# Moving the statistics of the time steps under the last projection tiles, and the rows of decay sums under the backward scan

## What is computed

```python
dt = jax.nn.softplus(dt_raw + dt_bias)
a = dt * (-jnp.exp(a_log))
acum = jnp.cumsum(ac, axis=2)
seg = acum[:, :, :, None] - acum[:, :, None, :]
lmat = jnp.exp(jnp.where(tril, seg, -jnp.inf))
y_diag = jnp.einsum('bclsge,bcsgep->bclgep', cb[..., None] * lmat, xc)
decay_to_end = jnp.exp(acum[:, :, -1:] - acum)
states = jnp.einsum('bcsgn,bcsgep->bcgepn', bc, decay_to_end[..., None] * xc)
```

## Time and profile before

| | |
|---|---|
| median of three runs | 3931.37 us |
| the profiled execution | 3925.94 us, its span 3924.3 us |
| PE busy | 3614.0 us (92%) |
| DVE, ACT, POOL busy | 2146.7, 1360.7, 1594.6 us |
| mean granted TensorE clock | 0.957 of 2.4 GHz |
| DMA | 521.87 MB, mean 133 GB/s |

### The profile page before, as it was taken

The page is one execution under the profiler, slowest core; times in us unless marked ns, Lnnn a source line. Parts: engine busy times, 40 slices in busy tenths (PEclk is TensorE's granted clock), DMA queues, the critical chain, the costliest instruction groups (busy, mean ns, idle before and its releaser), DMA issues. The chain is left out here.

```text
span 3924.3 us, 57718 instructions
## 1 busy us (share of the span) xinstructions
PE 3614.0 (92%) x20917; PEld 2850.7 (73%) x20917; DVE 2146.7 (55%) x4515; ACT 1360.7 (35%) x3566; POOL 1594.6 (41%) x1471
## 2 busy tenths in 40 slices
PE   6899999998875999899989998999999997899998
PEld 5777777887753667677767776677777775788887
DVE  2262145206414664366436653788888887465554
ACT  2122112212110003212322123778778885222222
POOL 5336342453505666567666664424233332100000
PEclk9999999999987999999999999999999998999999
DMA  4424422422314654634453342745544544444443
GB/s 166 150 77 138 170 77 72 136 94 64 102 40 160 212 166 137 209 122 136 128 185 120 122 142 89 172 125 136 137 127 114 139 132 128 162 158 154 166 152 103
DMA packets 366864, 521.87 MB, mean 133 GB/s; under 512 B 27595, under 2 KB 257555, under 8 KB 363859
## 3 DMA queue, kind: packets, MB, share of 16 engines
q1 hardware_dynamic: 329683, 402.80, 32.6%
q0 software_dynamic: 27456, 94.78, 8.1%
q10 hardware_dynamic: 9472, 20.97, 1.5%
HBM read 334.18 MB, written 184.29 MB: 132 GB/s over the span
## 5 line engine op out<-in xcount | busy, mean ns | idle before, releaser
L1713 ACT ACTIVATE attn_p_sb<-attn_p_sb,attn_o_sb 128x256 f32<-128x256 f32 (+1 forms) x1152 | 535.0, 466 | 183.7 <-DVE attn_o_sb L1747 178.2
L235 POOL TENSOR_TENSOR front_w_hi<-front_w_raw,one 128x1024 fp32r<-128x1024 f32 (+1 forms) x96 | 165.9, 1728 | 566.0 <-PE front_out L432 532.2
L1747 DVE CUSTOM_DVE_ANT_0 attn_p_sb<-attn_s_ps,attn_mask 128x256 f32<-128x256 f32 (+1 forms) x1152 | 368.8, 376 | 43.9 <-PE attn_s_ps L1646 43.7
L1067 PE MATMUL late_out<-h_hi,late_w_hi 128*128 128x512 f32 x1152 | 344.5, 443 | 22.5 <-issue 22.5
L1537 POOL COPY attn_q_apart<-attn_q 128x128 f32<-128x128 f32 (+2 forms) x256 | 136.9, 535 | 523.9 <-PE attn_s_ps L1646 517.5
L1067 PEld LDWEIGHTS late_out<-h_hi,late_w_hi 128*128 128x128 f32 x1152 | 225.0, 197 | 119.6 <-issue 78.4
L369 DVE TENSOR_SCALAR front_acc<-front_chan,front_consts 128x1024 f32<-128x1024 f32 (+2 forms) x36 | 38.8, 1077 | 473.3 <-ACT front_chan L281 473.3
L1186 ACT COPY late_m<-late_seg 128x512 f32<-128x512 f32 x96 | 55.9, 583 | 680.4 <-PE late_seg L1088 671.1
L1067 PE MATMUL late_out<-h_hi,late_w_lo 128*128 128x512 f32 x1152 | 286.7, 391 | 0.0
L1067 PE MATMUL late_out<-h_lo,late_w_hi 128*128 128x512 f32 x1152 | 284.5, 389 | 0.0
L1659 PE MATMUL attn_pt_ps<-ident,attn_p_sb 128*128 128x128 f32 x1920 | 278.4, 282 | 0.4 <-ACT attn_p_sb L1713 0.4
(11 more groups left out here) (211 smaller groups left out, 7380.1 us busy)
## 6 DMA issues: line engine op xcount, KB each, us to landing
front_w_raw<-w_in POOLq DMA_DIRECT2D x84, 512.0 KB, 4.1
output_parts<-s_o SPq DMA_DIRECT2D x24, 1584.0 KB, 6.5
late_w_raw<-w_in POOLq DMA_DIRECT2D x144, 256.0 KB, 3.9
s_o<-attn_o_sb SPq DMA_DIRECT2D x128, 264.0 KB, 3.0
late_xb<-s_xb SPq DMA_DIRECT2D x48, 640.0 KB, 5.8
s_zs<-front_stage SPq DMA_DIRECT2D x48, 256.0 KB, 2.0
s_v<-front_stage SPq DMA_DIRECT2D x48, 256.0 KB, 2.2
s_states<-late_state SPq DMA_DIRECT2D x24, 512.0 KB, 3.3
```

The costliest lines, as they stand in the source:

```text
L235: nc.gpsimd.tensor_tensor(hi, raw, one.to_broadcast([P, 2, cols]), ALU.mult).then_inc(sem["w_split"], 1)
L1067: last = nc.tensor.matmul(out[u][:, :], w[s][:, k, :], h[:, k, half], start=first, stop=h is h_lo and k == KT - 1)
L1713: last = nc.scalar.activation(cut, cut, ACT.Exp, scale=-1.0, bias=o_sb[g // 4 % ring][:, g % 4, h, VW:OW], accum_out=o_sb[g // 4 % ring][: ...
L1747: last = nc.vector.tensor_tensor_reduce(out=p_sb[g % 4][:, h, 0:width], in0=s_ps[g % 2][h][:, 0:width], in1=mask[:, step.pattern.strip(ste ...
```

## The change

- `ssd_stats_phase` and `decay_rows_phase` are gone as stages. dt stays on chip: it is no longer stored and loaded back.
- The statistics are computed in front_phase under the v units of the last block: DVE's part after its last work there, ACT's and PE's in single steps after named units (`STATS`, `SUMS`). Constant masks are set by POOL ahead of load 8. The four small loads of `dt_bias` and `a_log` go to SP's queue at the start. Results lie where x tiles and the norm's gain lay.
- The rows of sums are made in the backward slots: 12 rounds of 4 transposes instead of 6 of 8. Round r is filled by DVE in slot r + 2, turned by PE and copied by ACT in slot r + 3, split by DVE and stored by SP in slot r + 4.
- late_phase begins on POOL with the weights. The table of ones is made in five steps in slots 5, 7, 9, 11, 13. POOL weighs the first x between the first and the second weight. SP loads the rotation table ahead of the second x; `gain` and `skip` follow in slot 8.
- In slots 0 to 23 PE and DVE do the unit first and then the scan.
- The states of the backward scan go through three tiles instead of two.

```diff
+STATS = {("v", 0, 1): "exp", ("v", 0, 2): "log", ("v", 0, 6): "log_dt",
+         ("v", 1, 2): "decay", ("v", 1, 3): "entry", ("v", 1, 4): "total"}
+SUMS = {("v", 1, 0): 0, ("v", 1, 1): 1, ("v", 1, 2): 2}
...
             for load in range(BLOCKS * len(groups)):
+                if load == len(groups):
+                    set_masks()
...
+            def stats(what):
+                if what == "exp":
+                    act.wait_ge(sem["stats_in"], 16 * 2 * DIR)
+                    nc.scalar.activation(rate[:, :], a_log[:, :], ACT.Exp).then_inc(sem["stats_act"], 1)
...
+            def sums(i):
+                pe.wait_ge(sem["masks_set"], 9)
+                pe.wait_ge(sem["a_ready"], 1)
...
+                for d in range(DIR):
+                    last = nc.tensor.matmul((rest, upto, whole)[i][d], lhs[d], heads(a, d), start=True, stop=True)
...
-                    sp.dma_start(scratch["dt"][first:first + BLOCK, :].rearrange("(t p) n -> p t n", p=P),
-                                 dt_toks[:, :, :]).then_inc(sem["dt_stored"], 16)
...
-def ssd_stats_phase(nc, sem, c, params, scratch, st):
...
-def decay_rows_phase(nc, sem, c, scratch, st):
...
             fetch(0)
             fetch(1)
-            for w in range(2):
-                split(w)
+            split(0)
             weigh(0)
+            split(1)
             for slot in range(len(units)):
                 if slot + 1 < first_forward:
                     weigh(slot + 1)
+                if slot in (5, 7, 9, 11, 13):
+                    select_rows((slot - 5) // 2)
...
+            def store_rows(r):
+                sp.wait_ge(sem["wide_split"], r + 1)
...
             load_back(0)
+            sp.dma_start(table[:, :, :], t_in["rope"][:, :, BLOCK:]).then_inc(sem["l_rope_in"], 16)
             load_back(1)
...
                     store_back(slot)
+                    if 0 <= slot - first_round - 2 < rounds:
+                        store_rows(slot - first_round - 2)
...
+            def turn_rows(r):
+                pe.wait_ge(sem["wide_steps"], r + 2)
...
+                for k in range(4):
+                    last = nc.tensor.transpose(seg[r % 2][:, k * P:(k + 1) * P],
+                                               wide[r % 2][:, k, :, :].rearrange("p d n -> p (d n)"), c["ident"][:, :])
...
             for slot, unit in enumerate(units):
-                scan(slot)
-                multiply(unit)
+                if slot < first_forward:
+                    multiply(unit)
+                    scan(slot)
+                else:
+                    scan(slot)
+                    multiply(unit)
...
             def back_step(j):
                 dve.wait_ge(sem["b_state"], state_ready(j))
-                if j:
-
-                    dve.wait_ge(sem["b_stored"][1 - j % 2], 16 * ((j + 1) // 2))
...
+                if j >= 2:
+
+                    dve.wait_ge(sem["b_stored"][(j + 1) % 3], 16 * ((j + 1) // 3))
...
+            def fill_rows(r):
...
+                for part in range(2):
+                    last = nc.vector.tensor_copy(wide[r % 2][:, :, :, part * HEADS:(part + 1) * HEADS],
+                                                 source[:, first:first + 4, :].rearrange("p c (d h) -> p c d h", d=DIR))
...
+            def split_rows(r):
+                dve.wait_ge(sem["wide_high"], r + 1)
...
+                nc.vector.scalar_tensor_tensor(row_out[r % 2].bitcast(F32R), row_high[r % 2].bitcast(F32),
+                                               st["low_row"][:, :], seg[r % 2][:, :], ALU.mult, ALU.add
...
                 if slot < first_forward:
+                    if slot == first_round - 1:
+                        nc.vector.memset(y[:, :], 0.0).then_inc(sem["wide_steps"], 1)
...
+                    if 0 <= slot - first_round - 2 < rounds:
+                        split_rows(slot - first_round - 2)
+                    if 0 <= slot - first_round < rounds:
+                        fill_rows(slot - first_round)
                     back_step(slot)
```

More of the change, by code:

```diff
@@ L334, in _ @@
                     take_dt_back(unit, units[unit.n - 1].event)
+                if unit.b == BLOCKS - 1 and (unit.name, unit.part, unit.j) in STATS:
+                    stats(STATS[unit.name, unit.part, unit.j])
                 t = next_tile(unit)
@@ L467, in _ @@
                     turn_dt_back(unit, units[unit.n - 1].event)
+                if unit.b == BLOCKS - 1 and (unit.name, unit.part, unit.j) in SUMS:
+                    sums(SUMS[unit.name, unit.part, unit.j])
                 t = next_tile(unit)
@@ L774, in late_phase @@
     quads = HEADS // 4
+    rounds = 2 * NT // 4
+    first_round = 2
     units = late_units()
@@ L833, in state_ready, with rows_stored_before @@
             return j + 1 + (j >= turned_over)
+        def rows_stored_before(r):
+            return sum(DIR if x >= rounds // 2 else 1 for x in range(r % 2, r, 2))
         def part_of(slot):
@@ L965, in load_rows @@
                     sp.wait_ge(sem["f_rows_set"], 6)
+                    for u in range(2):
+                        sp.wait_ge(sem["sums_stored"][u], 16 * rows_stored_before(rounds + u))
                 sums = scratch["sums"].rearrange("(d q h) (c l) -> c d q h l", d=DIR, q=2, l=P)
@@ L1083, in decays @@
                     pe.wait_ge(sem["f_rows_in"], 48 * (n + 1))
+                    pe.wait_ge(sem["wide_split"], rounds)
                 pe.wait_ge(sem["f_m_steps"], n * (quads + 1) + q)
@@ L1163, in _ @@
         def _(act):
-            act.wait_ge(sem["f_rows_set"], 5)
-            nc.scalar.copy(rows[:, :, :], m[:, :, :]).then_inc(sem["f_rows_set"], 1)
             def load_h(turn, half):
@@ L1208, in _ @@
             for slot, unit in enumerate(units):
+                if 0 <= slot - first_round - 1 < rounds:
+                    high_rows(slot - first_round - 1)
+                if slot == first_round + rounds + 2:
+                    act.wait_ge(sem["f_rows_set"], 5)
+                    nc.scalar.copy(rows[:, :, :], m[:, :, :]).then_inc(sem["f_rows_set"], 1)
                 n, part = part_of(slot)
```

379 lines of the change are left out of this document (168 added, 211 removed).

## The result

The changed kernel takes 3897.62 us (median of 5 runs, 3883.20 to 3904.55), the kernel before 3931.37 in the same comparison: ratio 0.9912 [0.9898, 0.9926], 33.8 us saved where 57.7 were forecast. It is faster, and lies outside the range on the slow side. The profiled execution is the median one (span 3896.0 us).

A forecast was written before the change was run, and what follows sets the result against it. PE was taken to set the pace on both sides of its 86.1 us gap. Saving 67.4 at the begin, less 5.2 (rows), 2.5 (state load) and 2 (stalls), gave 57.7 us: 3931.4 to 3873.7 us, range 3853 to 3893.

The forecast's parts named there:

- the gap: PE's 86.1 us between front products and backward slots: predicted to become one stretch of some 12 to 18 us.
- three groups of sums: PE's statistics sums left after the last v units: 12 records at full clock, 3.9 us.
- the third tile: Third tile for the backward scan's states: worth nothing and costing nothing.
- the turning: PE's 12 rounds of four row transposes in the backward slots: 5.2 us given back, 10.4 at half clock.
- rival 2: POOL becomes the bound: weights late in slots 5 to 13, 15 us; 38 to 46 saved, near 3889; chance 0.17.
- rival 1: PE's stalls on DVE's state vanish in the backward slots: 70 to 79 us saved, near 3857; chance 0.15.
- rival 3: DVE's row copies collide with POOL every round, about 5 us each, 61 us: slower than before; chance 0.02.
- Begin: Last front product through slot 2: 42.2 us against 109.6, so 67.4 us saved, bounds 58 to 70.5.
- Slots 3 to 23: Backward slots: row transposes cost 5.2 us and stalls on DVE's state 2 us more.
- The stalls on DVE's state: 19 us lost in slots 3 to 23: pattern stays, 2 us more; bounds all 19 gone or 19 more.
- which unit stands between two `add_back`s: Unit before scan in backward slots only shifts this, 5.44 us in either order.
- Slot 25: After slot 24, PE waits for the backward state's load: 2.5 us lost, 0 if faster, 5 if the clock falls.

The follow-up runs named there:

- loads_in_turn: Changed kernel with the rotation table loaded after the first two weight pieces and chunk 0's states loaded ahead of x; 3887.62 us, ratio 0.9899.
- turned_in_psum: Changed kernel with the rotated halves of units 0 to 21 in two free PSUM banks instead of SBUF; 3869.86 us, ratio 0.9833.
- select_in_idle: Changed kernel with POOL's table of ones made in slots 2, 6, 10, 14, 18 instead of 5, 7, 9, 11, 13; 3886.34 us, ratio 0.9883.
- scan_first: Changed kernel with PE and DVE doing the scan before the unit in the backward slots, as before the change; 3884.95 us, ratio 0.9885.
- all five edits: Changed kernel with rotated halves in PSUM, selects moved, stores early, row copies on ACT, two loads later; 3856.22 us unit first, 3865.05 scan first.

## Why the prediction was right and wrong

**Right:** the gap was the place to gain, it was one stretch with one begin (14.6 us, within 12 to 18), DVE's and ACT's steps hid under v, three groups of sums took 4 us of PE, the third tile was worth nothing, the turning cost PE the 5.2 us taken (156.9 against 162.3 us of slots, with the old order and the rotation in PSUM, is 5.4). Of the rivals none came: PE waits for no low part of a weight in slots 5 to 13 (rival 2), stalls on the state are left (rival 1), and the copies cost PE only the two waits of 5.0 us (rival 3).

**Begin, 67.4 forecast, 57.0 measured: a mis-sized sum.** The weight's landing, taken as 5 us, was 8.46, near the bound of 8.9 from the table's own row; loads_in_turn shows that the table beside it costs 2.64 of it. Slots 0 to 2, 30 us from the landing, took 1196.8 - 1161.99 = 34.8; turned_in_psum, 6.6 us shorter from the first product on, shows that DVE's held rotation is the reason. The last front product ended 1.6 us later than the sums explain (the kernel before's own front code ended up to 3.1 us later in other kernels' profiles, so this need not be the change's), and the drain was 0.5 us longer: 3.5 + 4.8 + 1.6 + 0.5 = 10.4.

**Slots 3 to 23, 7.2 us more forecast, 13.1 measured: the step that failed.** Under "The stalls on DVE's state" the question "Does this stay?" was answered from L1258 alone, as POOL's doing, with 2 us for the new work; they grew by 7.9. And the order was to shift only "which unit stands between two `add_back`s". Both steps looked at PE and at one line of DVE. The rotation's second pair of operations also has two operands in SBUF, and in the kernel before 13.4 of the 19.1 us went when one of them was put into PSUM. The order matters as well: it decides whether PE waits for POOL's weighing, and what stands ahead of `back_step` on DVE. By the runs:

- the new order alone: 19.1 to 15.5 us, a gain of 3.6;
- with rows, copies and selects in slots 2, 6, ... (select_in_idle): 17.5;
- selects in the odd slots 5 to 13, as changed: 27.0, so 9.5 us for the place of five pieces of POOL's work (7.7 with the rotation in PSUM).

The prediction named these pieces, and looked only for a weight behind them. With the old order all of the new work would have cost 0.9 us (scan_first, 20.0 against 19.1): the 2 us taken fit an order that the change doesn't keep.

The Trainium skill (SBUF — State Buffer, section "SBUF: two separate sides") lists, beside the fp32 copy that the prediction cited, a VectorE operation with two SBUF inputs against a GpSimd operation that reads SBUF. The rows agree: L1238 takes 33.9 us for 21 operations with two; with one in PSUM 20 of them take 6.9 + 6.8 = 13.7. Applied to every line of DVE in the slots, the rule would have led to L1249 of the kernel before.

**Slot 25, 2.5 forecast, 6.3 measured: mis-sized.** PE waits 3.44 us, and then works at a granted clock of 0.60 (the mean of 1391.2 to 1397.2; 3.62 us for four products that take 1.88 at full clock). The upper end named, 5 for a fall of the clock, was nearer. loads_in_turn takes it away.

These make 10.4 + 5.9 + 3.8 = 20.1 us. By the medians 57.7 - 33.8 = 23.9 us are missing. The parts, however, are read from two profiled executions, which are only 28.3 us apart, so that 29.4 are missing there. Of the other 9.3 us 8.5 lie in the forward slots, whose code is the same, and 0.8 behind late_phase. From unit 29 to the end of late_phase the profiled execution of before took 965.1 us, that of the changed kernel 975.0. The other kernels took 967.2 to 975.7, and those made from the kernel before 966.0, 966.1 and 974.9, so that the kernel before's own code reaches either end. Whether a small part of this is the change's stays open.

## What to carry to other kernels

Before moving work, list every operation of the busy elementwise engine with both operands in SBUF, next to what POOL does in the same stretch: a wait is named after the last of them, here `back_step`, while the rotation before it had a share that its own length doesn't show. Put one operand into a free PSUM bank (13 and 14 us of slots here, in the two kernels) and long POOL work into slots in which POOL waits anyway (8 to 9.5 us). An order is not good or bad by itself: unit first won 3.6 and 4.5 us of slots in the kernel before and 5.4 with all five edits, and lost 7.0 and 6.9 with POOL's selects in the odd slots.

## What the runs showed of the hardware

A DVE operation that POOL holds up isn't always let in when POOL's instruction ends: the first of the two copies above lasts through a product of 1.91 us and the select of 2.01 us behind it, and L1248 at 1188.64 through two products of POOL. Nor is it only the one that comes second that waits, as the prediction read the earlier trace rows: the five long L1258 of the kernel before begin 0.63 us ahead of L886, each while POOL issues a fetch (at 1298.14 in the earlier trace rows, the issue from 1297.96 to 1298.75), and still last 4.63 us each, through L886 and the split behind it. POOL's instructions are held as well, less: the select of 2.0 us took 2.48 beside L1238. With an operand in PSUM no plain addition or multiplication (TENSOR_TENSOR) of 512 columns lasted over 0.70 us, and none of 1024 over 1.23, in these slots of the 18 profiled executions. And a 256 KB weight, landing 3.6 us after its issue in the median of the eight fetched up to 1188 us, took up to 9.5 with the table's and x's loads beside it.
